# A two-block transformer on one core: plain norms moved behind the product, the residual turned by halves, input and spatial stage reordered

## The reference, cut to what matters

```python
def rmsnorm(x, g):                       # x: 256 tokens x 1024, f32
    return x * rsqrt(mean(x * x, -1) + EPS) * g

# first block ("x" is the input, later the running sum h)
z = gelu(rmsnorm(h, a_norm_g) @ w_in); u, v = split(z, 2)       # w_in 1024 x 2048
v = rmsnorm(v, v_norm_g)
s = einsum('gij,bnjgc->bnigc', masked w_s, v) + b_s             # 8 groups, 128 x 128
h = h + (u * s) @ w_out
h = h + conv_ffn(rmsnorm(h, f_norm_g[0]))        # 1024 -> 2x2816, causal conv of 3, silu, -> 1024
kv = rmsnorm(h, kv_norm_g) @ w_kv
h = h + chunk_attention(rmsnorm(h, b_norm_g), k, v, w_q, rel_bias, w_o)
h = h + conv_ffn(rmsnorm(h, f_norm_g[1]))
x = rmsnorm(h, final_norm_g)
# second block: silu(c) @ ada_w + ada_b gives shifts, scales and gates; one layer with
# two attentions and a swiglu, one with sparse attention and 8 experts
```

## Time and profile before

| | us |
|---|---|
| median of 3 runs (1656.71 to 1658.23) | 1656.82 |
| the profiled execution | 1656.43 |
| its span | 1654.7 |
| PE / DVE / ACT busy in the span | 1496.4 / 1240.4 / 907.1 |
| chain that ended last: PE / DVE / ACT / issue / DMA | 69% / 17% / 6% / 5% / 1% |
| first matmul of a product | 25.67 |

### The profile page before, as it was taken

One profiled execution on the slowest core, in us unless ns is written; L12 is line 12 of the kernel. 1 busy time (PEld: TensorE's weight loads), 2 busy tenths in 40 slices (PEclk: granted clock), 3 DMA queues, 4 the chain that ended last, 5 costly groups with the idle time before them and its releaser, 6 DMA issues.

```text
span 1654.7 us, 19775 instructions
## 1 busy us (share of the span) xinstructions
PE 1496.4 (90%) x7242; PEld 1224.1 (74%) x7243; DVE 1240.4 (75%) x1695; ACT 907.1 (55%) x1147; POOL 4.2 (0%) x16
## 2 busy tenths in 40 slices
PE   5899999998899999787899998968699999999995
PEld 4778887776678878675788887746587788778874
DVE  4766888665758887567777785696488888888887
ACT  5545654443546553447433334445377777777774
POOL 0000000000000000000000000000000000000000
PEclk9989999998999999899899999979699999999997
DMA  8644446674234448361486774412178888878882
GB/s 325 229 148 162 173 184 252 255 295 183 82 150 153 189 163 313 149 254 52 153 290 249 262 290 161 152 51 77 43 284 314 302 337 308 322 288 342 305 314 102
DMA packets 54264, 358.16 MB, mean 216 GB/s; under 512 B 7088, under 2 KB 8112, under 8 KB 13360
## 3 DMA queue, kind: packets, MB, share of 16 engines
q1 hardware_dynamic: 51392, 353.47, 57.1%
q0 software_dynamic: 144, 2.10, 0.3%
q10 hardware_dynamic: 2656, 1.64, 0.3%
HBM read 356.13 MB, written 1.05 MB: 216 GB/s over the span
## 4 chain that ended last, share of the span: by engine, by line
PE 69%; DVE 17%; ACT 6%; issue 5%; DMA 1%; PEldq 0%; DVEq 0%; PEld 0%; ACTq 0%; SPq 0%
PE ps L422 21%; PE ps L424 20%; PE ps L423 20%; DVE wlo L1309 5%; PE ps L780 2%; ACT whi L923 2%; PE ps L533 1%; DMA head_scratch<-w_s_dram 1%; DVE tok L1856 1%; DVE tok L1444 1%; PE ps L557 1%; DVE attn_scratch L1533 1%; ACT ps L935 1%; DVE acc L1332 1%; ACT attn_scratch L1045 1%
## 5 line engine op out<-in xcount | busy, mean ns | idle before, releaser
L1309 DVE TENSOR_TENSOR wlo<-raw,whi 128x2048 fp32r<-128x2048 f32 (+1 forms) x303 | 651.1, 2171 | 190.4 <-ACT whi L923 178.2
L923 ACT ACTIVATE whi<-raw 128x2048 fp32r<-128x2048 f32 (+1 forms) x303 | 546.9, 1822 | 293.0 <-PE ps L424 292.6
L422 PE MATMUL ps<-whi,xhi 128*128 128x512 f32 (+3 forms) x1360 | 535.6, 394 | 22.8 <-DVE xlo L1389 8.0
L424 PE MATMUL ps<-whi,xlo 128*128 128x512 f32 (+3 forms) x1360 | 525.2, 386 | 0.0
L423 PE MATMUL ps<-wlo,xhi 128*128 128x512 f32 (+3 forms) x1360 | 525.1, 386 | 0.0
L422 PEld LDWEIGHTS ps<-whi,xhi 128*128 128x128 f32 x1360 | 259.6, 191 | 81.1 <-DVE wlo L1309 12.0
L424 PEld LDWEIGHTS ps<-whi,xlo 128*128 128x128 f32 x1360 | 259.1, 190 | 52.1
L423 PEld LDWEIGHTS ps<-wlo,xhi 128*128 128x128 f32 x1360 | 259.4, 191 | 47.9
L422 PE MATMUL ps<-whi,ahi 128*128 128x512 f32 x440 | 178.7, 406 | 11.7 <-DVE wlo L1309 11.7
L423 PE MATMUL ps<-wlo,ahi 128*128 128x512 f32 x440 | 175.4, 399 | 0.0
L424 PE MATMUL ps<-whi,alo 128*128 128x512 f32 x440 | 175.2, 398 | 0.0
(11 more groups left out here) (237 smaller groups left out, 1226.1 us busy)
## 6 DMA issues: line engine op xcount, KB each, us to landing
raw<-stream_dram SPq DMA_DIRECT2D x318, 1024.0 KB, 5.4
raw<-stream_dram SPq DMA_DIRECT2D x30, 512.0 KB, 4.2
attn_scratch<-toep_dram POOLq DMA_DIRECT2D x1, 2048.0 KB, 8.1
raw<-stream_dram SPq DMA_DIRECT2D x2, 528.0 KB, 3.7
h<-x_dram SPq DMA_DIRECT2D x1, 1024.0 KB, 5.3
y<-tok SPq DMA_DIRECT2D x2, 512.0 KB, 2.7
head_scratch<-w_s_dram ACTq DMA_DIRECT2D x1, 512.0 KB, 18.3
gates<-fg_dram ACTq DMA_DIRECT2D x1, 512.0 KB, 21.6
```

Source lines behind the costliest of these rows:

```text
L422: pe.matmul(o, xh, wh, start=start, stop=False)
L424: return pe.matmul(o, xl, wh, start=False, stop=stop)
L923: act.activation(whi[:, q % SPL, 0:w], raw[:, s % RAW, 0:w], ACT.Copy).then_inc(sem("hi_done"), 1)
L1309: dve.tensor_tensor(wlo[:, q % SPL, 0:w], raw[:, s % RAW, 0:w], whi[:, q % SPL, 0:w].bitcast(F32), ALU.subtract).then_inc(sem("lo_done"), 1)
```

## The change

1. **Norm behind the product.** For gmlp_in, up0, kv, q and up1, x is h times the gain only. The inverse root goes on the sums as ACT takes them: one instruction per tile of tokens with `scale=st[:, 6 + t]` (`by_tile`, `take_scaled`), 2 of 512 columns where there was 1 of 1024. DVE makes no normalised copy there; squares go to TA in SBUF instead of PSUM.
2. **Residual by halves.** h's blocks 0 to 3 are final when the first half's sums are added. PE turns them ahead of the last slot of the second chunk (`lead`), blocks 4 to 7 after the first tile of the next product's first slot (`rest`). ACT and DVE follow with `residual_then`: between DVE's last addition and the second half of x stands the split of the next product's second slot. The same for gmlp_out, down0 and attn_out; not behind down1. q's x is made by halves around kv's last slot.
3. **Input stage.** PE turns x itself as soon as it has landed; statistics come behind; ws is turned behind the first chunk.
4. **Spatial stage.** The spatial product stands behind the first slot of the fourth chunk, its gate and transposes by halves inside that chunk's second slot and gmlp_out's first.
5. **Modulation.** The two "a" slots of gmlp_in move to the end of up0; all in between keep their number.

In the diff the first `residual_then` is ACT's, the second DVE's; `squares`, `roots`, `moments` and `inverses` are the parts that `stats` and `normalise` were made of.

```diff
-        proj("gmlp_in", 2 * D, G_ORDER, layer=0, first=4)
+        proj("gmlp_in", 2 * D, G_ORDER)
         proj("gmlp_out", D, layer=0)
-        proj("up0", 2 * FF)
+        proj("up0", 2 * FF, layer=0, first=18)
...
+            def lead(slots):
+                def after(j):
+                    if j == slots - 2:
+                        pe.wait_ge(sem("acc_free"), T("acc"))
+                        two(h, 0)
+                        two(h, 1)
+                return after
+            def rest(n):
+                def mid(j):
+                    if j == 0:
+                        pe.wait_ge(sem("h_added"), NT * n)
+                        two(h, 2)
+                        two(h, 3)
+                return mid
...
+            tail(h)
+            x_ready()
+            proj(W)
             pe.wait_ge(sem("ws_landed"), 16)
...
+            proj(W, mid=gated(0, 1), after=spatial)
             x_ready()
+            proj(W, mid=gated(2, 0))
+            proj(W, early=True, after=lead(2))
+            gated_ffn(4, rest(1), lead(6))
             x_ready()
-            norm_tail(TA)
-            gated_ffn(4)
-            norm_tail(TA)
-            x_ready()
...
+            proj(W, mid=rest(2), after=lambda j: two(h, 0) if j == 1 else None)
...
+            attention(CHUNKED, "attn_out", SM_C, PT_C, lead(2))
+            gated_ffn(4, rest(3))
...
+            def by_tile(dst, src, func):
+                for t in range(NT):
+                    m = act.activation(dst[:, t], src[:, t], func, scale=st[:, 6 + t:7 + t])
+                return m
...
+            def residual_then(gain, kt=KT):
+                used[0] += len(slots_of(kt, W))
+                split(used[0] + AHEAD)
+                next_pair()
+                used[0] += len(slots_of(kt, W))
+                split(used[0] + 1)
+                next_pair()
+                tail(xT_c, gain, rounds=(0, 1))
+                split(used[0] + 2)
+                T.up("acc", 2)
+                squares(h)
+                tail(xT_c, gain, rounds=(2, 3))
+                act.activation(st[:, 26:27], ones[:, 0:1], ACT.Sqrt)
+                roots()
+                act.wait_ge(sem("rinv"), T.up("rinv", NT))
...
                 used[0] += slots
                 split(used[0] + 1)
+                if lead:
+                    tail(xT_c, (0, 1))
...
+            def residual_then(kt=KT):
+                residual(kt=kt, lead=True)
+                split(used[0] + 2)
+                moments()
+                tail(xT_c, (2, 3))
+                inverses()
```

More of the change, by code:

```diff
@@ L465, in second_half, with down @@
                         late_x[0] = False
-                product(width, KT, xhi, xlo, at_slot=second_half, early=early, after=after)
-            def down(kt, late):
+                product(width, KT, xhi, xlo, at_slot=second_half, early=early, mid=mid, after=after)
+            def down(kt, late, after=None):
                 made = [0]
@@ L536, in transposes, with gated_ffn @@
                 T.up("tr")
-            def gated_ffn(n_tr):
+            block_of = lambda src, k: (lambda t: src[:, t, k * P:(k + 1) * P])
+            two = lambda src, r: rounds([block_of(src, 2 * r), block_of(src, 2 * r + 1)], first=r)
+            def lead(slots):
[12 more added lines that the diff above has]
+                return mid
+            def gated_ffn(n_tr, mid=None, after=None):
                 n = FK // 2
@@ L541, in gated_ffn @@
                 for j in range(n):
-                    proj(W)
+                    proj(W, mid=None if j else mid)
                     if j:
                         transposes(n_tr)
-                down(FK, lambda: transposes(n_tr))
+                down(FK, lambda: transposes(n_tr), after)
             turned = [0]
@@ L627, in groups @@
                         pe.wait_ge(sem("att_o"), bg + 4)
-                product(W, KT, xhi, xlo, at_slot=groups, mid=lambda: values(n - 1))
-                product(W, KT, xhi, xlo, early=True)
+                product(W, KT, xhi, xlo, at_slot=groups, mid=lambda j: None if j else values(n - 1))
+                product(W, KT, xhi, xlo, early=True, after=after)
             pe.wait_ge(sem("consts"), 1)
+            pe.wait_ge(sem("x_landed"), 16)
+            tail(h)
+            x_ready()
+            proj(W)
@@ L644, in _ @@
[L644 to L650, removed]
-            x_ready()
-            for c in range(2):
-                proj(W, early=c)
@@ new lines, in spatial @@
+            def spatial(j):
+                if j == 0:
+                    pe.wait_ge(sem("vn_ready"), NT)
+                    pe.wait_ge(sem("wsT_ready"), 2)
+                    pe.wait_ge(sem("acc_free"), 3)
+                    for g in range(KT):
+                        pe.matmul(ps[:, (0, 1, 4, 5)[g // 2], (g % 2) * S:(g % 2 + 1) * S].rearrange("p (t c) -> p t c", t=NT),
+                                  wsT[:, g, :], TB[:, :, g * P:(g + 1) * P], start=True, stop=True).then_inc(sem("spatial"), 1)
@@ L665, in _ @@
+            proj(W, after=lambda j: two(h, 1 + j))
+            proj(W, after=lambda j: two(h, 3) if j == 0 else None)
             proj(W)
@@ L1476, in conv_ffn @@
                 convolve(n - 1)
-                residual(kt=FK)
             def turn_in(j, f):
@@ L1591, in _ @@
             dve.sem_inc(sem("conv_used"), 1)
-            normalise(h, TA)
+            tail(xT_c, (0, 1))
             split(2)
-            dve.wait_ge(sem("wsT_ready"), 1)
-            dve.memset(wsT[DH:P, :, 0:DH], 0.0).then_inc(sem("wsT_ready"), 1)
-            tail(xT_c)
+            tail(xT_c, (2, 3))
+            moments()
+            inverses()
             skip(1)
```

154 lines of the change are left out of this document (87 added, 67 removed).

## The result

The changed kernel takes **1628.76 us** (median of 4 runs, 1628.06 to 1630.92), the kernel before 1656.76 on the same chip: a ratio of 0.9832, 95% interval 0.9819 to 0.9844. That is 28 us faster, where 39 were predicted; the time lies 0.8 us above the top of the range. The profiled execution has 1629.31 us with a span of 1627.6, so 27.1 us less in the span.

The account below looks back on a forecast made before the run. PE was taken as the bound inside products, so only its waits could be gained: 16.6 + 7.8 + 5.4 + 6.3 + 7.0 - 3.7 - 0.2 = 39.2 us, giving 1617 us; range 1609 to 1628.

Parts of the forecast that it names:

- The start, 16.6: From kernel start to gmlp_out's last addition: ends at 89.1 instead of 105.7, 16.6 us gained.
- the bound on the constants: At the start: last constant lands at 31.3, slot 5's split ends at 38.3, leaving 0.7 us before PE's third chunk.
- rival 1: DVE the new wait at passages: 10.5 us, plus 2.5 for late constants, 13 in all, 1630; chance 0.20.
- The first condition that the text named for being wrong: At the start: the first product held at its fifth slot by the constants for more than 3 us.
- Passages, 7.8, 5.4 and 6.3: From DVE's last residual addition to the next product's first chunk: gains of 7.8 us at up0, 5.4 kv, 6.3 up1.
- q, 7.0: At q: PE's 5.45 us wait for x and 1.5 of lower clock go, 7.0 us gained.
- up0's end, 3.7: At the end of up0: two modulations moved there push DVE's convolution back, 3.7 us lost.
- Takes, 0.2: Two 512-column takes replacing one of 1024: covered by ACT's idle time except at q's last chunk, 0.2 us lost.
- Rival 2: In products with inserted transposes: 10 groups each lower the clock and lose 1.5 us, 15 in all, 1632; chance 0.05.
- Rival 3: From 15 to 620 us: PE without rests gets a lower clock; at 0.94 all 39 us are lost; chance 0.03.
- Rival 4: More gained: up0's end modulations half hidden and PE starting warm, 3 to 8 us more, 1612 to 1609; chance 0.12.

Follow-up runs that it names:

- experiment 1: Changed kernel with the router's table rw on a semaphore of its own, awaited only ahead of the router's product: median 1623.54 us.
- experiment 2: Changed kernel with SyncE issuing the ninth and later weight slots only once the four small loads have landed: median 1625.46 us.
- experiment 4: Changed kernel with up0's two modulations behind its slots 3 and 5 instead of 19 and 21: median 1629.74 us.

## Why the prediction was wrong, point by point

- **The start, 16.6, was 8.3.** The steps up to the first matmul (14.9, measured 15.03) held. The step that failed is the bound on the constants: "The last of them lands at 4.0 + 27.3 = 31.3". It took a landing time from the kernel before into a start in which the weights run ahead of it. The text named the danger ("because the loads of two further slots share the engines"), priced it right (each us beyond 0.7 costs one) and put it in rival 1 as 2.5 us; it was 5.9 late, 5.2 after the slack. With PE's later arrival at that chunk (0.5), the stall is 5.2, the lower clock on the chunk behind adds 2.0, and the rest up to the last addition 0.6: 8.3. Experiments 1 and 2 give back 5.9 and 4.8 of it, so this step is shown for 5.9 of the 12.1 missing us. The other 2.4 of the stage stay when the constants are on time: the second chunk is taken 0.8 late (39.77, predicted 39.0), the fourth starts 1.8 after the predicted 49.9 (51.69; 0.7 of that is the wait behind ACT and the split, for which the sum had no term), and 0.6 come behind it. The first condition that the text named for being wrong, the fifth slot held for over 3 us by the constants, is what happened.
- **Passages, 7.8, 5.4 and 6.3.** Right in mechanism: no wait on a normalised copy, a gap under 0.5 before the second slot at up0, 1.29 in kv where 1.6 was predicted. At up0 and up1 the whole is 13.1 instead of 12.5: 0.23 are the gap, the rest is spread over restarts behind the inserted groups. Together they brought 0.6 less at each of the two, 0.2 less at kv.
- **q, 7.0**: 7.1. Right in mechanism and size.
- **up0's end, 3.7.** Its stage lost 5.2, of which 0.8 are the leading transposes. The modulations themselves cost 2.7 (experiment 4). Two terms were missing or too small: the sum that PE makes for the moved pair (0.8, at 229.87) and the takes.
- **Takes, 0.2**: 1.7 us. The longer take was to be covered by idle time everywhere but at q; it is not covered in the 22 chunks of up0 and up1. The bounds had been 0.2 to 1.2, too narrow, because they counted only places where ACT is the bound.
- **Rival 1** gave 1630, and the result is 1628.8, but that is luck. Its three late passages, 10.5 of its 13 us, did not come: the gaps there are under 0.5 and 1.29. Only its 2.5 for late constants did, at more than twice that price; the rest of the shortfall has the other causes of this list.
- **Rivals 2 and 3** fell: 118 to 232 and, with experiment 1, all of 16 to 60 ran at 1.00, transposes included; no rest was needed. **Rival 4** had the modulations half hidden: 1 of their 3.7 us was.
- **The second block** was taken as fixed. It took 987.6 to 991.7 us in the profiled executions of one and the same code; in the pairs that were compared the difference arose where the granted clock differed. That is as large as the last terms of the sum, and belonged into the range.

## What to carry to other kernels

When a change makes an engine start earlier, every transfer that was "just in time" for the old start has to be priced anew, with the loads that the earlier start itself sets off: the landing time of a small table is not its own property. Let a wait cover only the transfers that the waiting engine uses; splitting it off changed nothing in the kernel before (1657.2 against 1656.7) and gave 5 us in the changed one. When the first wait of a stage is removed, ask which engine's chain stands next: here it was ACT's, and PE waited 0.7 us behind it. Before a transfer is moved behind others on a compute engine's queue, look at how long the issue itself holds the engine.

## What the runs showed of the hardware

- A 32 KB table took 22.1, 27.3, 33.0 or 34.2 us from issue to landing in variants of one program, depending on the weight loads beside it.
- An issue of 512 KB as the sixth on ScalarE's queue, behind three tables, held the engine for 17.36 us; the same transfer on SyncE's queue, issued at 17.4, took 0.43. The 32 KB table took 2.30 as sixth issue and 0.76 as fifth. That the first had to wait for room in the queue is argued, not shown.
- A stall of 5.2 us cost 2.0 us more on the chunk behind it, by the clock; where the stall was removed the clock stayed at 1.00.
- One stretch of short matmuls was granted 1.00 in some kernels and 0.66 in others with identical instructions there, 3.4 us in the time.
- Two takes of 512 columns take 1.16 us from start to the next instruction where one of 1024 takes 0.92, and PE's chunk grows by 0.12 in each second one.
